# Expert stage of a two-block model: row transfers by quarters, the scatter's signal in two halves, another order of loads for the third tile, and the last router products with their operands exchanged

## What is computed

```python
p_group = softmax(x32 @ wg + bg); pg, g_sel = top_k(p_group, 1)          # 4 groups
e_in = (x32 @ we + be).reshape(t, 4, 8)[chosen group]                    # 8 experts in a group
top_v, top_i = top_k(e_in, 2); gates = softmax(top_v) * pg
ids = (g_sel * 8 + top_i).reshape(-1); order = argsort(ids); tok = order // 2
xs = xf[tok]                                                             # 2048 rows, sorted by expert
hg, hu = ragged_dot(xs, w_gate, sizes), ragged_dot(xs, w_up, sizes)      # 1024 -> 512 each
ys = ragged_dot(silu(hg) * hu, w_down, sizes)                            # 512 -> 1024
y = segment_sum(ys * gates, tok)
```

## Time and profile before

| | |
|---|---|
| median of 3 runs | 4153.5 us (4152.88 to 4157.52) |
| the profiled execution | 4154.1 us, its span 4152.3 us |
| mean granted TensorE clock | 0.934 of full speed |
| TensorE busy | 87% of the span |
| VectorE, ScalarE busy | 68%, 39% |
| DMA | 689.49 MB moved |
| largest DMA groups | 68 + 68 + 66 halves of expert weights, 1 MB each |

### The profile page before, as it was taken

How to read it: one execution, slowest core, us unless ns; L and a number is a source line. 1 busy time by engine, 2 the same in 40 slices (tenths; PEclk the granted TensorE clock), 3 DMA queues, 4 the chain that set the end, 5 groups by cost and what they waited for, 6 DMA issues and landing times. The chain is left out here.

```text
span 4152.3 us, 62374 instructions
## 1 busy us (share of the span) xinstructions
PE 3627.6 (87%) x24735; PEld 2922.9 (70%) x24735; DVE 2834.9 (68%) x3463; ACT 1610.1 (39%) x2136; POOL 71.9 (2%) x56
## 2 busy tenths in 40 slices
PE   6999996879969999947999776649999897999897
PEld 4888885767758888835888532319997676888786
DVE  4775325977569999977886588695555657666455
ACT  3222212545437777743333120253333134323244
POOL 0000000000020000010000000000000000000000
PEclk8999998999969999968999888779999998999998
DMA  5942225536579999952333331340111332222565
GB/s 195 337 169 92 88 77 198 186 124 216 178 282 421 414 411 408 381 188 86 118 112 112 118 127 63 122 156 28 49 34 58 100 124 76 82 83 80 187 194 166
DMA packets 270498, 689.49 MB, mean 166 GB/s; under 512 B 38136, under 2 KB 134072, under 8 KB 243754
## 3 DMA queue, kind: packets, MB, share of 16 engines
q1 hardware_dynamic: 234474, 559.76, 37.5%
q10 hardware_dynamic: 20528, 67.11, 4.3%
q0 software_dynamic: 15248, 59.14, 3.9%
HBM read 530.81 MB, written 172.96 MB: 169 GB/s over the span
## 5 line engine op out<-in xcount | busy, mean ns | idle before, releaser
L156 PE MATMUL g_ps<-h1T_hi,g_w_lo 128*128 128x512 f32 x448 | 175.6, 392 | 7.1 <-DVE g_w_lo L355 7.1
L1771 DVE TENSOR_TENSOR moe_wg_lo<-moe_wg,moe_wg_hi 128x2048 fp32r<-128x2048 f32 x68 | 153.1, 2288 | 35.6 <-ACT moe_wg_hi L1625 35.6
L158 PE MATMUL g_ps<-h1T_hi,g_w_hi 128*128 128x512 f32 x448 | 175.0, 391 | 0.0
L157 PE MATMUL g_ps<-h1T_lo,g_w_hi 128*128 128x512 f32 x448 | 175.0, 391 | 0.0
L1771 DVE TENSOR_TENSOR moe_wu_lo<-moe_wu,moe_wu_hi 128x2048 fp32r<-128x2048 f32 x68 | 152.9, 2288 | 15.9 <-ACT moe_wu_hi L1625 15.9
L4142 DVE TENSOR_TENSOR x3T_lo<-fd_w_raw,x3T_hi 128x1024 fp32r<-128x1024 f32 x66 | 80.8, 1224 | 120.5 <-ACT x3T_hi L4071 120.4
L156 PE MATMUL g_ps<-x2T_hi,g_w_lo 128*128 128x512 f32 x352 | 140.1, 398 | 24.7 <-DVE g_w_lo L582 24.7
L1771 DVE TENSOR_TENSOR moe_wd_lo<-moe_wd,moe_wd_hi 128x2048 fp32r<-128x2048 f32 x66 | 148.3, 2289 | 15.4 <-ACT moe_wd_hi L1625 15.4
L2860 PE MATMUL rs_banks<-rs_pm,rs_qx 64*64 64x64 f32 x2048 | 157.2, 217 | 0.0
L156 PE MATMUL fd_acc<-x3T_hi,x3T_lo 128*128 128x512 f32 x352 | 139.6, 397 | 18.4 <-DVE x3T_lo L4145 18.4
L156 PE MATMUL g_ps<-g_w_hi,h1T_lo 128*128 128x512 f32 x384 | 149.6, 390 | 0.0
(11 more groups left out here) (734 smaller groups left out, 10768.0 us busy)
## 6 DMA issues: line engine op xcount, KB each, us to landing
moe_wg<-in_exp_w_gate SPq DMA_DIRECT2D x68, 1024.0 KB
moe_wu<-in_exp_w_up SPq DMA_DIRECT2D x68, 1024.0 KB
moe_wd<-in_exp_w_down SPq DMA_DIRECT2D x66, 1024.0 KB
fd_w_raw<-in_ffn_w_down SPq DMA_DIRECT2D x66, 512.0 KB, 4.5
go_w_raw<-in_w_out SPq DMA_DIRECT2D x64, 512.0 KB, 4.3
g_w<-in_w_in SPq DMA_DIRECT2D x52, 512.0 KB, 4.6
g_w<-in_w_in SPq DMA_DIRECT2D x22, 1024.0 KB, 7.7
s_xs<-g_zero POOLq DMA_DIRECT2D x2, 8192.0 KB, 34.3
```

The source lines that it names most:

```text
L156: pe.matmul(out, l[1], r[0], start=(k == 0), stop=False)
L157: pe.matmul(out, l[0], r[1], start=False, stop=False)
L158: return pe.matmul(out, l[0], r[0], start=False, stop=(k == kt - 1))
L1771: v.tensor_tensor(lo[:, q * m:q * m + m], w[:, q * m:q * m + m], hi[:, q * m:q * m + m], ALU.subtract).then_inc(sem_lo, 1)
```

## The change

**Rows by quarters.** Row counts for each tile are worked out on VectorE (`fill`, `step_w`, `left`) and put behind the old table in `tile_exp`; `rows_ok` tells that they are there. The load of a tile's rows on SyncE and the store of its results on ScalarE's queue each become four DMAs of 32 rows, each done only if the tile has a row in that quarter. For this both queues read the row count from the table in each step. All counts of `x_in` and `stored` are multiplied by four. Because unwritten rows of `ys` stay, all of `ys` is now filled with zeros in the early `gemm`, where before its first 2048 rows were left out.

**Scatter in two halves.** The transfers of tokens 0 to 511 count on `moved[0]`, those of 512 to 1023 on `moved[1]`. ScalarE's first `wd_hi` waits for `moved[0]` alone, VectorE's first `wd_lo` for `moved[1]`, and SyncE's load of the rows of tile 2 for both.

**Third tile's weights first.** On SyncE step 1 is written out as well. In it the gate and up weights of tile 2 are loaded first, and only then come the waits for `turned`, `rows_ok` and the scatter, and the rows of tile 2.

**Last router products.** For the tokens of the last pair the 36 router columns are the stationary operand and the 128 tokens the moving one. The result (36 x 128) is copied by ScalarE to `pair`, and turned back by TensorE.

```diff
@@ moe: the loads on SyncE
+            def rows_x(j, b):
+                n_rows = sp.value_load(tile_exp[0:1, bass.ds(j + (ROW_AT + 1), 1)], min_val=0, max_val=SEQ)
+                if isinstance(j, int):
+                    for m in moved:
+                        sp.wait_ge(m, 16 * NT)
+                for q in range(NX):
+                    o = slice(q * ROWS, q * ROWS + ROWS)
+                    sp.dma_start(x[o, 1 - b], xs.rearrange("(j p) n -> j p n", p=P)[j + 1, o],
+                                 cond=(n_rows > q * ROWS)).then_inc(x_in[1 - b], 16)
...
-                if not first:
+                if not isinstance(j, int):
                     sp.wait_ge(turned, past(j))
-                    sp.dma_start(x[:, 1 - b], xs.rearrange("(j p) n -> j p n", p=P)[j + 1],
-                                 cond=(n_used > j + 1)).then_inc(x_in[1 - b], 16)
+                    rows_x(j, b)
                 for q in range(2):
                     sp.wait_ge(g_lo, past(j * 2 + (q + 1)))
                     weights(g_in, wg, w_gate, e1, j + 1, new1, q)
                 for q in range(2):
                     sp.wait_ge(u_lo, past(j * 2 + (q + 1)))
                     weights(u_in, wu, w_up, e1, j + 1, new1, q)
+                if isinstance(j, int) and j == 1:
+                    sp.wait_ge(turned, past(j))
+                    sp.wait_ge(rows_ok, past(1))
+                    rows_x(j, b)
...
-                if isinstance(j, int) and j == 0:
-                    sp.wait_ge(moved, 16 * 2 * NT)
...
-            steps(sp, 1, step)
+            steps(sp, 2, step)
@@ moe: the store on ScalarE's queue
-                    act.wait_ge(moved, 16 * 2 * NT)
+                    act.wait_ge(moved[0], 16 * NT)
...
-                    act.dma_start(ys.rearrange("(j p) n -> j p n", p=P)[j - 1], y[:, 1 - b]).then_inc(stored[1 - b], 16)
+                    n_rows = act.value_load(tile_exp[0:1, bass.ds(j + (ROW_AT - 1), 1)], min_val=0, max_val=SEQ)
+                    for q in range(NX):
+                        o = slice(q * ROWS, q * ROWS + ROWS)
+                        act.dma_start(ys.rearrange("(j p) n -> j p n", p=P)[j - 1, o], y[o, 1 - b],
+                                      cond=(n_rows > q * ROWS)).then_inc(stored[1 - b], 16)
@@ moe: VectorE
-            v.drain()
+            v.memset(fill[:, E:], 0.0)
+            v.drain()
+            v.scalar_tensor_tensor(fill[:, 0:E], start[:, :], float(P), p_c, ALU.mult, ALU.add)
...
+            v.tensor_tensor(step_w[:, :], fill[:, 1:], fill[:, 0:E], ALU.subtract)
+            v.drain()
+            v.tensor_tensor(big, big, bc(step_w[:, :].unsqueeze(1), [P, N_LIST, E]), ALU.mult)
+            v.drain()
+            v.tensor_reduce(left[:, :], big, AXX, ALU.add)
...
+                if first:
+                    v.wait_ge(moved[1], 16 * NT)
                 low(d_hi, d_lo, wd, wd_hi, wd_lo, j + 1)
@@ deep_norm: the router's last pair on TensorE and ScalarE
-                for t in passes[-1]:
-                    rate(t)
+                for i, t in enumerate(passes[-1]):
+                    pe.wait_ge(by_dve, past(t + 1))
+                    for k in range(ND):
+                        mm = products3(pe, acc[0:nf, t % n_acc, 0:P], [h[:, k] for h in (f_hi, f_lo)],
+                                       [h[:, t % 2, k] for h in (t_hi, t_lo)], k, ND)
+                    mm.then_inc(pair_done, 1)
+                for i, t in enumerate(passes[-1]):
+                    pe.wait_ge(pair_ok, past(i + 1))
+                    mm = pe.transpose(pl[:, t, 0:nf], pair[0:nf, t % 2], ident[0:nf, 0:nf])
+                mm.then_inc(rated, 1)
...
+                for i, t in enumerate(g):
+                    act.wait_ge(pair_done, past(i + 1))
+                    act.activation(pair[0:nf, t % 2], acc[0:nf, t % n_acc, 0:P], ACT.Copy).then_inc(pair_ok, 1)
```

More of the change, by code:

```diff
@@ L1435, in moe @@
     KD, KF = D // P, D_EXP // P
-    N0, NA = 64, 2
+    N0, NA, NX = 64, 2, 4
+    ROWS, ROW_AT = P // NX, 2 * N_LIST + 1
     bg, be, io, ids = consts
@@ L1459, in moe @@
         token = s.sb("token", [P, NA], U32)
+        fill, step_w, left = s.sb("fill", [P, E + 1]), s.sb("step_w", [P, E]), s.sb("left", [P, N_LIST])
         p_x, p_g, p_u, p_a, p_y = (s.ps("p_x", [P, KD, P]), s.ps("p_g", [P, D_EXP]), s.ps("p_u", [P, D_EXP]),
@@ L1464, in moe @@
                          p_route[:, 512 - 2 * NA:512])
-        pre, exps, hots, ranks, slot_ok, head_ok, here_ok, found, token_ok, table_ok = (s.sem(n) for n in (
-            "pre", "exps", "hots", "ranks", "slot_ok", "head_ok", "here_ok", "found", "token_ok", "table_ok"))
+        pre, exps, hots, ranks, slot_ok, head_ok, here_ok, found, token_ok, table_ok, rows_ok = (s.sem(n) for n in (
+            "pre", "exps", "hots", "ranks", "slot_ok", "head_ok", "here_ok", "found", "token_ok", "table_ok", "rows_ok"))
         w_in = [s.sem(f"w_in{n}") for n in "gud"]
-        moved = s.sem("moved", soft=True)
+        moved = [s.sem(f"moved{n}", soft=True) for n in range(2)]
         x_first = [s.sem(f"x_first{j}", soft=True) for j in range(NA)]
@@ L1600, in step @@
                     pe.wait_ge(x_first[1], 16)
-                pe.wait_ge(x_in[1 - b], past((k2 + b) * 16 + 16))
+                pe.wait_ge(x_in[1 - b], past((k2 + b) * (16 * NX) + 16 * NX))
                 turn_rows(1 - b)
@@ L1618, in _ @@
             for b in range(2):
-                act.nop().then_inc(stored[b], 16)
+                act.nop().then_inc(stored[b], 16 * NX)
             def high(sem_in, sem_hi, w, hi, n):
@@ L1780, in _ @@
             low(u_hi, u_lo, wu, wu_hi, wu_lo, 1)
+            v.tensor_tensor(step_w[:, :], fill[:, 1:], fill[:, 0:E], ALU.subtract)
[4 more added lines that the diff above has]
+            v.drain()
+            v.scalar_tensor_tensor(left[:, :], io[:, 0:N_LIST], -float(P), left[:, :], ALU.mult, ALU.add)
+            v.drain()
+            v.tensor_scalar(tile_exp[:, ROW_AT:], left[:, :], fill[:, 0:1], 0.0, ALU.add, ALU.max).then_inc(rows_ok, 1)
             def step(j, b, k, n_used):
@@ L1795, in step @@
                     v.wait_ge(downed, past(j))
-                    v.wait_ge(stored[1 - b], past((k + b) * 16))
+                    v.wait_ge(stored[1 - b], past((k + b) * (16 * NX)))
                     v.tensor_copy(y[:, 1 - b, 512:], p_y[:, 512:]).then_inc(y_dve, 1)
+                if first:
+                    v.wait_ge(moved[1], 16 * NT)
                 low(d_hi, d_lo, wd, wd_hi, wd_lo, j + 1)
@@ L1809, in _ @@
                     pool.indirect_dma_start(xs[:, :], bass.IndirectOffsetOnAxis(ap=slots[:, k, t:t + 1], axis=0),
-                                            h2_rows[:, t], None).then_inc(moved, 16)
+                                            h2_rows[:, t], None).then_inc(moved[t // (NT // 2)], 16)
 def combine_norm(nc, ys, gate2, slots, x, w, ident, hT, x14, x2, y_out, hy_w, hy_b, mu, par):
@@ L3910, in deep_norm @@
             pt, pl = s.ps("pt", [P, ND, P]), s.ps("pl", [P, NT, 64])
-            f_high, f_low, turned, by_act, by_dve, rated = (s.sem(n) for n in (
-                "f_high", "f_low", "turned", "by_act", "by_dve", "rated"))
+            f_high, f_low, turned, by_act, by_dve, rated, pair_done, pair_ok = (s.sem(n) for n in (
+                "f_high", "f_low", "turned", "by_act", "by_dve", "rated", "pair_done", "pair_ok"))
+            pair = s.sb("pair", [P, 2, P])
             few_in = s.sem("few_in", soft=True)
@@ L4219, in _ @@
                     low(t)
-                v.wait_ge(rated, past(NT))
+                v.wait_ge(rated, past(NT - 1))
                 v.tensor_copy(logits[:, :, :], pl[:, :, 0:nf])
@@ L4333, in first_layer @@
                 dict(kind="tok", post="centre", w=w_in[:, O_V:O_V + ML_W], out=vo[:, 0:ML_W]),
-                dict(kind="tok", post="sigmoid", w=w_in[:, O_O:O_O + ML_W], out=vo[:, ML_W:])], clear=(scratch("xs")[0:N_TILE * P], ys[SEQ * 2:]), aside=work)
+                dict(kind="tok", post="sigmoid", w=w_in[:, O_O:O_O + ML_W], out=vo[:, ML_W:])], clear=(scratch("xs")[0:N_TILE * P], ys), aside=work)
     x1, h2 = scratch("x1", [SEQ, D]), scratch("h2", [SEQ, D])
@@ L4351, in first_layer @@
     tabs.close()
-    tile_exp = chosen.enter_context(nc.sbuf_tensor("tile_exp", [P, 2 * N_LIST + 1], I32))
+    tile_exp = chosen.enter_context(nc.sbuf_tensor("tile_exp", [P, 3 * N_LIST + 1], I32))
     xs, x2 = scratch("xs"), scratch("x2", [SEQ, D])
```

13 lines of the change are left out of this document (7 added, 6 removed).

## The result

The changed kernel takes 4169.5 us, the median of 7 runs (4161.3 to 4179.2), beside 4153.0 us before (7 runs, 4151.7 to 4157.5). The ratio is 1.0043, with a 95% interval of 1.003 to 1.0055. The forecast was 4152.6 us in 4146 to 4168, with 0.21 for slower. The time lies 1.5 us above the range, on the side that had a fifth of the chance.

What follows compares the result with a forecast made beforehand. TensorE was taken to bound the steady step at 17.91 us, with 17.4 us of transfers beneath. Terms -3.4 + 0.3 + 1.7 + 0.5 = -0.9 us on 4154.1, the median 0.6 lower: 4152.6 us, range 4146 to 4168.

Steps and rivals of the forecast that it cites:

- Fewer rows moved: Expert stage's steps: 0.40 MB of 7.34 MB left out, 0.95 us if transfer-bound, taken as 0 because TensorE sets the step.
- rival C: Expert stage's steps: transfers are the bound after all, 31 steps gain up to 0.95 us, 4123 us; chance 0.05.
- Rival B: ScalarE's queue overruns and the Silu gets later until TensorE waits, say 1 us a step, 4183 us; chance 0.07.
- What the quarters cost on ScalarE: Table read and quarter stores before each Silu: Silu 0 to 0.6 us late, hidden by 3.0 us to spare, taken as 0.
- What the quarters cost on SyncE: One table read and three DMAs more, about 2.5 us a step in SyncE's queue, hidden in its idle time: 0.
- Start: Expert stage's start: weights delay the scatter's end by 10.0 us, most is given back later, up products +1.7 us.
- Rival D: Expert stage's start: scatter keeps priority, -2.4 in place of +1.7, 4148.5 us; 0.70 together with the forecast.
- Router: Last router products: 48 exchanged products at 120 ns, not 213, save 4.5 us; with copy and transposes -3.4 us.
- Rival A: Router: short moving operands cost several cycles a column, 427 ns a product, 4166.8 us in all; chance 0.15.
- End of the stage: ScalarE's last store and skipped steps begin about 2 us later: 0 to +1.5, taken as +0.5 us.

Runs made afterwards that it cites:

- e6: e3 with each quarter's row load spread over every fourth partition, stores still whole: 4152.7 us.
- e4: The changed kernel with row loads and stores both whole again, without their table reads: 4150.7 us.
- e3: The changed kernel with stores on ScalarE whole again, no table read there, row loads still in quarters: 4184.9 us.
- e9: e3 with each quarter's row load put in every second partition of one half of 64: 4181.0 us.
- e12: e3 with row loads in two conditional halves of 64 neighbouring rows in place of quarters: 4190.2 us.
- e2: The changed kernel with row loads on SyncE whole again, no table read there, stores still in quarters: 4152.0 us.
- e7: e2 with the stores' quarters spread over every fourth partition: 4162.2 us.
- e10: e4 with the third tile's rows loaded ahead of its gate and up weights: 4143.8 us.
- e11: e5 with the scatter in two halves and SyncE's wait for it moved directly ahead of tile 2's rows: 4148.5 us.
- e5: The kernel before with only the router's exchanged products: 4148.9 us.

## Why the prediction was wrong

**Fewer rows moved: wrong, and the failed step.** It was put as "I take 0", since the step is TensorE's. That the rows left out gain nothing held: with the loads spread, e6 has e4's step of 17.95 us. What failed is that the quarters' loads would cost the DMA nothing. The sum went over bytes alone and took it that a byte costs the DMA the same in any transfer. With 17.4 us of transfers under 17.91 there was half a microsecond to lose. Row loads that stay in one half of the partitions have packets of 250 to 290 ns, not 159, slow the weights' packets beside them, and so made the step transfer-bound: 18.67 us in the profiled execution, 22.7 us more over 30 steps. The 0.95 us that the left-out quarters are worth at the full rate did not make up for that. e6 and e3 show it with one edit, e9 and e12 show which property of the transfer it is. Neither rival C (transfers are the bound, and fewer bytes gain) nor B was this: the transfers did become the bound, and it cost.

**What the quarters cost on ScalarE: right in the changed kernel as a cause by itself, with no margin left.** The parts were sized well (table read up to 0.8 us against 0.63 to 0.80 measured, the issues of the quarters 1.8 us against 1.73). e2 shows that this is hidden as long as the weights are in time. But the cover was taken to be VectorE's 3 us; in truth the work stands in a loop of ScalarE and VectorE, and some 0.35 us of slack was left. Rival B's mechanism is real: e7 brings it out with 0.45 us more a step, and it costs 0.26 us a step. Its point of decision, 4 us of added queue work, was wrong: it lies at 17.91 us for the loop. Most of the 42.5 us put down to issue in the changed kernel follow from the late weights: with whole loads and the same stores (e2) it is 6.9 us.

**What the quarters cost on SyncE: right**, 0 as far as its queue goes. e6 has all of it and a step of 17.95.

**Start: mechanism right.** The scatter gives way to the weights: 9.1 us later, where 10.0 were predicted. The gate products have no wait. The third Silu is 2.3 us later than before, where 1.7 and the slots' 0.3 were predicted, within the 2 us by which executions differ. That the order is a bad one showed only against e10 and e11. Rival D (the scatter keeps its priority) is refuted. Its own figures give the prediction 1247.6 for the up products (1242.1 + 5.5), not 1247.9, so the term was 1.4.

**Router: right in direction, too small.** -3.4 was predicted, -5.4 measured in the changed kernel and in e5. The 48 products take 4.1 us (1148.53 to 1152.65, with a wait of 0.4 between the two tiles) in place of 10.0, and the copy and transposes behind them add 0.5, where 1.1 were taken. At the low clock the pitch is 0.107 us, below the 120 ns taken; the rest is the clock, which rose to 1.00 under the exchanged products, while before it stayed at 0.50 from 1145 to 1156 us, to the end of the old ones. Why it rose here wasn't tested. Over the thirteen traces with the exchange the stretch is 10.2 to 11.2 us, 16.5 before. Rival A (4 cycles a column) is refuted; its 4166.8 left out the +0.5 of the stage's end, and the lower bound of -4.1 is -4.0 by its own 107 ns.

**End of the stage: too small.** +0.5 was predicted, +1.8 measured. From the last `wd_lo` to `nf_taps` are 7.1 to 7.2 us before, in e4 and in e3, and 8.9 to 9.8 in the kernels that store by quarters: it is the stores' share.

**What stays open.** Why the weights' packets slow down beside such loads, and why neighbouring stores don't slow down at all. The 4.6 us between the medians of e10 and e11. And 0.04 us a step, 1.2 us in all: with the changed expert stage the kernels whose weights are in time and whose stores are whole (e4, e6, e10) have steps of 17.95 us, and before, e5 and e11 have 17.91. The difference lies mostly in the gate products, whose code is the same.

## What to carry to other kernels

Before cutting a load into conditional pieces, look at what partitions a piece covers: a piece that stays in one half of the 128 partitions can cost more than the whole, and a quarter spread over every fourth partition does not. Neither form of the quarters gained anything here, since the step was TensorE's. Where the DMA share is 1 and TensorE is only just the bound, price transfers by their time and not by their bytes. And before putting a table read and issues into a compute engine's queue, close the loop through the engines that wait for each other: its length against the step decides, not the idle time beside the added work.

## What the runs showed of the hardware

- A DMA share of about 1 says nothing of the rate: 274 GB/s at a share of 1.00 and 434 GB/s at 1.09 stand two microseconds apart.
- A packet of 4 KB of a load took 159 ns when the load covered both halves of the partitions, and 250 to 290 ns when it stayed in one half. A packet of a store took 159 ns either way.
- Four conditional issues of which two move rows take 2.18 us of ScalarE's queue when the rows are spread over every fourth partition, and 1.73 when they are neighbours; when all four move rows it is 2.83 and 2.2. One whole store takes 0.34.
- Products with 36 stationary and 128 moving columns stand 0.107 us apart at the granted clock of 0.50 (1.2 GHz) and 0.06 at 1.00 (2.4 GHz). With 128 stationary and 36 moving columns they stood 0.213 us apart at 0.50.
